# Projections of a hybrid backbone: weight sums on VectorE, the convolution in two buffers loaded a quad ahead, bank copies ahead of its sigmoid

## The chip, the core and the metric

The kernel runs on one core of a Trainium2 chip. The metric is device time in microseconds. The engines are TensorE (PE; its weight loads are PEld), VectorE (DVE), ScalarE (ACT), GpSimd (POOL) and SyncE (SP), which here issues the DMAs of the projections.

## The reference

A two-layer backbone over 256 context and 2048 latent tokens, width 1024, all in float32. In each layer one input projection feeds four head groups, whose outputs are concatenated and projected back. What the change touches is the projection and what is computed beside it:

```
h = rmsnorm(x, norm_g) * (1 + scale) + shift
s = split_cols(h @ w_in)               # 1024 -> all segments, DEPTH = 2 layers
xbc = silu(dwconv_centred(s["ss_xbc"], conv_w, conv_b))    # 3 taps over the tokens, 768 channels
q, k = apply_rope(s["da_q"]), apply_rope(s["da_k"])         # latent tokens
z  = silu(gate segments)
logf, kk = forget gate and key of hg_f, from log_sigmoid
```

## The kernel before

**Products.** `projection(k, l)` runs once a layer. The 18 token tiles are taken in nine pairs, three pairs to a group, and the columns of w_in in five blocks. A *quad* is (group g, block b, member j): one pair of tiles, one block. The order is groups, in them blocks, in them the three members, 45 quads. Each quad is a 2 x 2 block product by seven products instead of eight (Winograd's form): P1 into bank A, P6 into B, P7 into D, P5 into E, then P2 on top of A, P4 on top of D, P3 on top of E. Each product is 4 matmul calls, which the trace shows as 8 instructions. Blocks 0, 1, 2 and 4 have 512 columns (wide quads), block 3 has 268 (narrow quads). In the last layer the context's pair needs plain products of a few columns only; those five quads (0, b, 0) are `simple`.

**Weight sums.** The form needs sums of the four weight quarters: T1 and T2 (`t12`, VectorE, at the end of a block's last quad for the next block), T3 (written over B12; `t3`, GpSimd) and T4 (`t4`, GpSimd). T3 is used by P7, T4 by P4. The sums S1 to S4 of the inputs are GpSimd's (`sums`).

**Bank copies.** ScalarE copies P1 out of bank A (`p1`, L805); only then may TensorE add P2 (its fifth product). When P2 is in, ScalarE copies bank A to the result (L825; L821 in plain quads), and only then may the next quad's P1 start. VectorE adds banks B, D, E and the parts: yy, ff, c22, c21, c12 (L945 to L974). Between them it does, in stages 1 to 4, the elementwise work of the quad before: the forget gate of block 1, the rotation of block 2, the gating.

**Convolution.** The depthwise convolution is cut in 72 jobs over both layers, half of 768 channels by one token tile each. A job is: SP loads three shifted copies of xbc and now and then bias and filter (L497 to L501); GpSimd multiplies and adds in three instructions (L633 to L635); ScalarE makes the sigmoid in three (`conv_gate`: L741, L742, L770); VectorE multiplies into `co` (L967, L978); SP stores (L491). There is one buffer `cx`, and SP loads a job's taps after the product of the job before. `CONV[q]` names the jobs of a quad. They begin in a group's block 1, member 1, and cover all quads to its block 4; some have two.

**Order.** Each engine runs its own instructions in program order and waits on semaphores. In a quad ScalarE does: gates of the quad before, copy L805, `between`, `normalise` where pairs turn, `after`, sigmoid of the quad's first job, copy L825, sigmoid of its second. SP does: the next block's weights (4 MB, first quad of a block, L354), store and taps of the first job, results of the quad before, store and taps of the second.

Of the kernel before, what the change touches and what calls it, by code (L numbers as in the profile page):

```python
# [22 lines left out]
ALU = mybir.AluOpType  # L23
# [3 lines left out]
P = 128  # L27
# [25 lines left out]
XBC = 768  # L53
# [318 lines left out]
def projection(k, l):  # L372
# [30 lines left out]
    CONV_TILES = [range(0, 5), range(5, 11), range(11, NT)]  # L403
    CONV = {q: [] for q in range(N)}
    jobs = []
    for g in range(GROUPS):
        some = [(g, c, t) for c in range(2) for t in CONV_TILES[g]]
        slots = [quad_of[g, b, j] for b in range(1, NB) for j in range(MEMBERS)][1:]
        if g == GROUPS - 1:
            slots = slots[:-1]  # L410
        extra = [quad_of[g, b, j] for b, j in ((3, 0), (3, 1), (3, 2), (4, 0))][:max(0, len(some) - len(slots))]
        for job, q in zip(some, sorted(slots + extra)):
            CONV[q].append(len(jobs))
            jobs.append(job)
# [20 lines left out]
    with ExitStack() as c:  # L435
# [11 lines left out]
        rp = k.sb(c, "rp", [P, NT, 3, 16])  # L447
        cx = k.sb(c, "cx", [P, 4, CWD])
        cw = k.sb(c, "cw", [P, 3, CWD])
        co = k.sb(c, "co", [P, CWD])  # L450
# [6 lines left out]
                      "lf_neg lf_log lf_key kk_ready lf_neg2 lf_log2 lf_done st_u0 st_u1 st_kk taps_in weights_in "  # L457
                      "conv_step conv_sum conv_sig conv_done st_conv act_step dve_step zero_made zero_rows")
# [17 lines left out]
        with nc.Block() as program:  # L476
            @program.sync
            def _(sp):
# [6 lines left out]

                def taps(m):
                    g, c, t = jobs[m]
                    part = slice(c * CWD, c * CWD + CWD)
                    if m:
                        sp.wait_ge(s["conv_done"], m)  # L490
                        sp.dma_start(k.xc[jobs[m - 1][2], :, jobs[m - 1][1] * CWD:(jobs[m - 1][1] + 1) * CWD], co[:]) \  # L491
                            .then_inc(s["st_conv"], 16)
                    q = quad_of[g, 0, 2]
                    sp.wait_ge(s[f"st_u{q % 2}"], stored(q))
                    sp.wait_ge(s[f"st_u{(q - 1) % 2}"], stored(q - 1))
                    for a in range(3):
                        sp.dma_start(cx[:, a], k.xbc[t + 1, a:a + P, part]).then_inc(s["taps_in"], 16)  # L497
                    if m == 0 or jobs[m - 1][1] != c:
# [78 lines left out]
                for q in range(N):  # L577
# [3 lines left out]
                    if CONV[q]:  # L581
                        taps(CONV[q][0])
# [2459 lines left out]
```

## Time and profile before

| | us |
|---|---|
| median of 3 runs | 5803.46 (5801.42 to 5803.72) |
| profiled execution, its own time | 5811.81 |
| its span | 5809.9 |
| PE busy | 5185.6 (89%) |
| DVE busy | 2776.0 (48%) |
| POOL busy | 2750.6 (47%) |
| ACT busy | 1831.9 (32%) |
| mean granted PE clock | 0.935 |
| first to last product, layer 0 | 90.77 to 1191.96 |
| first to last product, layer 1 | 3005.56 to 4123.38 |

The busy share of TensorE is an average over stages. What the projections lose is read from the stretches in which TensorE isn't busy, and from the clock there: 1.00 is 2.4 GHz.

### The profile page before, as it was taken

How to read it: one execution, taken by the hardware profiler on the slowest of the kernel's cores; microseconds unless marked ns; L12 is line 12 of the kernel's file. 1: busy time of each engine (PE TensorE's matmuls, PEld its weight loads, DVE VectorE, ACT ScalarE, POOL GpSimd, SP SyncE). 2: the span in 40 equal slices, each digit the busy share in tenths (PEclk: the TensorE clock that was granted, in tenths of full speed). 3: DMA queues.
4: the chain of work that ended last, by engine and by line, in shares of the span. 5: the costliest groups of instructions: out<-in, count | busy, mean ns of one | idle time of the engine just before them, and what ended most of it. 6: DMA issues, size and time to landing. Idle time of an engine off the chain costs nothing. (4 is left out here: it accounts for less than half of the span.)

```text
span 5809.9 us, 68743 instructions
## 1 busy us (share of the span) xinstructions
PE 5185.6 (89%) x25272; PEld 2736.5 (47%) x25272; DVE 2776.0 (48%) x4578; ACT 1831.9 (32%) x4021; POOL 2750.6 (47%) x1746
## 2 busy tenths in 40 slices
PE   6989899778888899998988898997688879999989
PEld 2454444446777433332434544444467763333334
DVE  2433434335777655551334335353357766555324
ACT  1222222222434244443112222222224432444422
POOL 1333343413344299997113333434134434999941
PEclk8999999877999799998999998998779998999999
DMA  5343433365222100001433333333362211000022
GB/s 185 130 138 131 133 133 130 110 203 176 96 89 75 52 1 8 8 6 71 152 112 121 134 131 127 132 120 110 119 201 83 98 49 46 1 8 8 5 113 104
DMA packets 410015, 559.17 MB, mean 96 GB/s; under 512 B 102840, under 2 KB 281840, under 8 KB 405328
## 3 DMA queue, kind: packets, MB, share of 16 engines
q1 hardware_dynamic: 389954, 514.36, 26.6%
q10 hardware_dynamic: 19728, 40.41, 1.8%
q8 instruction: 203, 3.33, 0.2%
q14 instruction: 130, 1.06, 0.1%
HBM read 400.32 MB, written 154.06 MB: 95 GB/s over the span
## 5 line engine op out<-in xcount | busy, mean ns | idle before, releaser
L2434 POOL TENSOR_TENSOR attention_PS<-attention_PS 128x1024 f32<-128x1024 f32 x548 | 1266.0, 2353 | 80.5 <-ACT attention_PS L2567 73.3
L2480 DVE TENSOR_REDUCE attention_mxp<-psum 128x1 f32<-128x512 f32 (+1 forms) x1016 | 654.7, 686 | 541.9 <-PE psum L2617 541.9
L2567 ACT ACTIVATE attention_PS<-psum 128x512 f32<-128x512 f32 (+1 forms) x1168 | 630.9, 592 | 717.5 <-PE psum L2671 700.3
L2617 PE MATMUL psum<-attention_QK 32*128 32x512 f32 (+1 forms) x2592 | 771.8, 611 | 9.1 <-DVE attention_mxp L2469 6.1
L667 PE MATMUL psum<-group_B,projection_hT 128*128 128x512 f32 (+1 forms) x1360 | 598.6, 587 | 180.9 <-ACT projection_u L825 91.8
L2665 PE MATMUL psum<-attention_QK 32*128 32x512 f32 x2336 | 664.7, 643 | 0.0
L2683 PE MATMUL psum<-attention_PS,attention_va 128*64 128x512 f32 x2336 | 627.7, 616 | 0.0
L667 PE MATMUL psum<-group_B,projection_S 128*128 128x512 f32 (+1 forms) x1360 | 564.2, 558 | 24.6 <-issue 10.4
L667 PE MATMUL psum<-projection_T,projection_S 128*128 128x512 f32 (+1 forms) x1360 | 560.8, 556 | 0.0
L633 POOL TENSOR_TENSOR projection_cx<-projection_cx,projection_cw 128x1152 f32<-128x1152 f32 x72 | 195.6, 2717 | 726.2 <-DMA projection_cx<-xbc 534.1
L667 PEld LDWEIGHTS psum<-group_B,projection_hT 128*128 128x128 f32 x1360 | 276.3, 206 | 464.2 <-issue 393.8
L667 PEld LDWEIGHTS psum<-group_B,projection_S 128*128 128x128 f32 x1360 | 260.9, 192 | 301.2 <-issue 273.9
L667 PEld LDWEIGHTS psum<-projection_T,projection_S 128*128 128x128 f32 x1360 | 262.9, 193 | 273.2 <-issue 260.8
L2665 PEld LDWEIGHTS psum<-attention_QK 32*128 32x128 f32 x2336 | 181.1, 184 | 444.8 <-issue 400.2
L609 POOL TENSOR_TENSOR group_B<-group_B,group_B 128x2048 f32<-128x2048 f32 (+1 forms) x30 | 166.1, 5537 | 407.2 <-DVE projection_T L839 385.9
L1759 POOL TENSOR_TENSOR mixing_Xk<-mixing_E,mixing_hkT 128x256 f32<-128x256 f32 x238 | 191.3, 804 | 314.9 <-ACT mixing_E L1826 307.3
L2617 PEld LDWEIGHTS psum<-attention_QK 32*128 32x128 f32 x2592 | 304.2, 189 | 75.6 <-DVE attention_mxp L2469 42.5
L2683 PEld LDWEIGHTS psum<-attention_PS,attention_va 128*64 128x64 f32 x2336 | 115.9, 135 | 354.3 <-issue 325.1
L667 PE MATMUL psum<-projection_T,projection_hT 128*128 128x512 f32 (+1 forms) x680 | 280.3, 555 | 1.6 <-DVE projection_ff L951 1.6
L2103 PE MATMUL psum<-mixing_mats,mixing_hg 128*128 128x128 f32 x1904 | 280.7, 291 | 0.0
L1826 ACT ACTIVATE mixing_E<-psum 128x512 f32<-128x512 f32 x238 | 141.5, 595 | 414.4 <-PE psum L2103 412.9
L2103 PEld LDWEIGHTS psum<-mixing_mats,mixing_hg 128*128 128x128 f32 x1904 | 235.4, 194 | 29.0 <-issue 0.9
(396 smaller groups left out, 7659.6 us busy)
## 6 DMA issues: line engine op xcount, KB each, us to landing
group_B<-in_w_in SPq DMA_DIRECT2D x120, 512.0 KB, 7.1
group_B<-in_w_in SPq DMA_DIRECT2D x48, 1024.0 KB, 8.9
projection_cx<-xbc SPq DMA_DIRECT2D x216, 192.0 KB, 3.1
u<-projection_u SPq DMA_DIRECT2D x158, 256.0 KB
mixing_hg<-u SPq DMA_DIRECT2D x34, 1024.0 KB, 5.0
u<-projection_u SPq DMA_DIRECT2D x52, 512.0 KB
output_y<-y SPq DMA_DIRECT2D x34, 512.0 KB, 4.1
xc<-projection_co SPq DMA_DIRECT2D x72, 192.0 KB, 2.1
```

Of the source, the lines that this page charges most:

```text
L609: TT(b12[:, :, 0:w], b22[:, :, 0:w], b12[:, :, 0:w], ALU.subtract).then_inc(s["t3_made"], 1)
L633: st.then(TT(cx[:, 0:3], cx[:, 0:3], cw[:], ALU.mult))
L667: ins = nc.tensor.matmul(bank[n][:, 0:w], left[:, q], right[:, q, 0:w], start=(first and q == 0), stop=(q == HK - 1), skip_group_check=True)
L1759: G.tensor_tensor(skew(Xk[v % 2][:], 0, [[w, 2], [2 * w, P // w], [1, w]]), skew(E[v % 2][:], 0, [[256 + w, 2], [2 * w, P // w], [1, w]]), ...
L1826: bk.release(A(out, bk[job][:, 0:w], func), job)
L2103: ins = T(bk[job][:, i * P:(i + 1) * P], hcol(t, "hg_f", i * P, P), m, start=True, stop=True)
L2434: G.tensor_tensor(SA[x % 2][:, rs, 0:w], one[:, rs, 0:w], PT[i % PTB][:, rs, 0:w], ALU.add) \
L2480: bk.release(V.tensor_reduce(mxp[x % 2][:, q:q + nn, 2 * pr + j, a], bk[job, j][:, 0:nn * (hi - lo)].rearrange("p (q n) -> p q n", q=nn), ...
L2567: bk.release(A(PT[i % PTB][:, r, 0:w], bk["st", i, r][:, 0:w], ACT.Exp, scale=scale), ("st", i, r))
L2617: return T(out[:, at:at + hi - lo], QK[rows(r), a0, t * P:(t + 1) * P], QK[rows(r), 2 + a0, lo:hi], start=True, stop=True)
L2665: T(o_, QK[rows(r), 2 + a0, kt * P:(kt + 1) * P], QK[rows(r), a0, t0 * P:(t0 + nq) * P], start=True, stop=False)
L2683: ins = T(k.bank[4 + j][64 * m:64 * m + 64, 0:w], va[:, kts[n], 2 * halves[x][1] + j], PT[i % PTB][:, r, 0:w], start=(n == 0), stop=(n == ...
```

## The change

Three things. T3 and T4 are made by VectorE: T3 of the next block between the bank sums c21 and c12 of a block's last quad, T4 between ff and c22 of a block's first. The convolution gets two buffers and its own table of places, `CONV_SLOTS`; a job's taps are loaded in the quad before it if the job two before is more than a quad back (`ahead`), else in its own quad; VectorE multiplies in place, at the end of the quad; the filter has its own wait. ScalarE copies bank A before all sigmoids of the quad. Beside it the rotation's table is loaded by group, and block 1's stage 2 stands before yy.

```diff
+    CONV_SLOTS.append([(1, 1, 1), (1, 1, 2), (1, 2, 0), (1, 2, 1), (1, 2, 2), (1, 3, 0),
+                       (1, 4, 0), (1, 4, 1), (1, 4, 2), (2, 0, 0), (2, 0, 1), (2, 0, 2)])
+    CONV_SLOTS.append([(2, 1, 1), (2, 1, 2), (2, 2, 0), (2, 2, 1), (2, 2, 2), (2, 2, 2), (2, 3, 0),
+                       (2, 3, 1), (2, 3, 2), (2, 4, 0), (2, 4, 0), (2, 4, 1), (2, 4, 1), (2, 4, 2)])
...
+    new_weights = lambda m: m == 0 or jobs[m][1] != jobs[m - 1][1]
+    new_bias = lambda m: m < 2 or jobs[m][1] != jobs[m - 2][1]
+    ahead = lambda m: m < 2 or at_quad[m - 2] < at_quad[m] - 1
...
-        cx = k.sb(c, "cx", [P, 4, CWD])
+        cx = many("cx", 2, [P, 4, CWD])
...
                 def taps(m):
-                    if m:
-                        sp.wait_ge(s["conv_done"], m)
-                        sp.dma_start(k.xc[...], co[:]).then_inc(s["st_conv"], 16)
...
+                    if m >= 2:
+                        sp.wait_ge(s[f"st_conv{m % 2}"], 16 * (m // 2))
...
+                def weights(m):
+                    at_least(sp, s["conv_sum"], m)
+                    sp.dma_start(cw[:], ...).then_inc(s["weights_in"], 16)
...
-                    if CONV[q]:
-                        taps(CONV[q][0])
+                    for m in CONV[q - 1] if q else ():
+                        conv_store(m)
+                    for m in CONV[q]:
+                        if not ahead(m):
+                            taps(m)
                     if q:
                         store(q - 1)
...
+                    for m in CONV[q + 1] if q + 1 < N else ():
+                        if ahead(m):
+                            taps(m)
+                        if new_weights(m):
+                            weights(m)
...
-                if not last:
-                    t3(0)
                 sums(0)
-                t4(0)
...
-                    for m in CONV[q][:1]:
-                        conv_gate(m)
                     at_least(act, s[f"st_u{q % 2}"], stored(q - 2))
...
                         A(u[q % 2][:, 0, 0:w], bank["A"][:, 0:w], ACT.Copy).then_inc(s["free_A"], 1)
-                    for m in CONV[q][1:]:
+                    for m in CONV[q]:
                         conv_gate(m)
...
+                    if first_of(q) and q:
+                        dve.wait_ge(s["product"], products(q))
+                        t4(i)
...
+                    if last_of(q) and q + 1 < N and not simple(q + 1):
+                        t3(i + 1)
...
+                    for m in CONV[q]:
+                        conv_multiply(m)
```

In the order tables the names are those of the program: p is the copy of P1, e the gates' scratch. ScalarE, layer 0, block 3 of group 1, its first quad and the start of the second; before:

```order
L805 ACTIVATE projection_p<-psum 128x268
L741 ACTIVATE projection_cx<-projection_cx 128x384
L742 ACTIVATE projection_cx<-projection_cx 128x384
L770 ACTIVATE projection_cx<-projection_cx 128x384
L825 ACTIVATE projection_u<-psum 128x268
L741 ACTIVATE projection_cx<-projection_cx 128x384
L742 ACTIVATE projection_cx<-projection_cx 128x384
L770 ACTIVATE projection_cx<-projection_cx 128x384
L741 ACTIVATE projection_e<-projection_u 128x1024
```

The same place now:

```order
L819 ACTIVATE projection_p<-psum 128x268
L837 ACTIVATE projection_u<-psum 128x268
L754 ACTIVATE projection_cx<-projection_cx 128x384
L755 ACTIVATE projection_cx<-projection_cx 128x384
L784 ACTIVATE projection_cx<-projection_cx 128x384
L754 ACTIVATE projection_e<-projection_u 128x1024
```

The copy of bank A (L837) has moved ahead of the sigmoid, and one job instead of two stands in this quad.

SP, layer 0, quad (2,3,0), from the weights of block 4 to the store of the quad before; before:

```order
L354 DMA group_B_3<-in_w_in 128x4x512
L491 DMA xc<-projection_co 128x384
L497 DMA projection_cx<-xbc 128x384 x3
L508 DMA u<-projection_u 128x2x512
L508 DMA u<-projection_u 128x2x256 x2
```

The same place now, on to the filter's load:

```order
L354 DMA group_B_3<-in_w_in 128x4x512
L519 DMA xc<-projection_cx 128x384 x2
L507 DMA projection_cx<-xbc 128x384 x3
L530 DMA u<-projection_u 128x2x512
L530 DMA u<-projection_u 128x2x256 x2
L507 DMA projection_cx<-xbc 128x384 x3
L509 DMA projection_cx<-in_ss_conv_b 128x384
L514 DMA projection_cw<-in_ss_conv_w 128x3x384
```

Two stores stand ahead of the taps of this quad's own job (whose L507 waits for the first of the two to land), and the taps and filter of the next quad's job follow.

VectorE, layer 0, quad (2,3,2), the last narrow quad; now (T3 is written to group_B_1):

```order
L978 TENSOR_TENSOR projection_yy<-psum,projection_p 128x268
L909 TENSOR_TENSOR projection_u<-projection_u,projection_e 128x4x256
L984 TENSOR_TENSOR projection_ff<-psum,projection_yy 128x268
L994 TENSOR_TENSOR projection_u<-psum,projection_ff 128x268
L851 TENSOR_TENSOR projection_T<-group_B_1,group_B_0 128x2048
L854 TENSOR_TENSOR projection_T<-group_B_3,projection_T 128x2048
L1004 TENSOR_TENSOR projection_u<-psum,projection_yy 128x268
L859 TENSOR_TENSOR group_B_1<-group_B_3,group_B_1 128x2048
```

L859 is new on this engine; L851 and L854 (T1, T2) stand where they did.

## Rows read from the trace of the kernel before

**Rows 1.** Line L667: what ended the idle time ahead of it (us, times).

```profile
  ACT projection_u L825: 91.8, 14
...
  ACT projection_p L805: 91.8, 12
```

**Rows 2.** Stretches: length, busy PE, PEld, DVE, ACT, POOL, PEclk, DMA share, GB/s.

```profile
312.31:369.38 57.07, 40.01 (x169) 32.83 (x168) 23.37 (x28) 16.00 (x25) 22.00 (x10) 0.88 0.52 170
664.80:734.01 69.21, 43.45 (x170) 34.63 (x168) 22.32 (x29) 17.45 (x28) 26.52 (x13) 0.83 0.47 152
1027.73:1130.16 102.43, 62.99 (x193) 43.86 (x192) 31.31 (x35) 24.02 (x38) 45.58 (x20) 0.77 0.39 124
3148.49:3180.76 32.27, 13.33 (x42) 8.37 (x41) 20.36 (x16) 9.18 (x13) 13.35 (x5) 0.74 0.51 156
3225.39:3282.78 57.39, 36.87 (x178) 31.59 (x176) 19.14 (x22) 12.66 (x24) 21.45 (x10) 0.76 0.48 158
3584.05:3652.27 68.22, 44.64 (x170) 35.35 (x168) 21.02 (x29) 17.45 (x28) 26.53 (x13) 0.80 0.45 151
3956.97:4061.58 104.61, 63.57 (x193) 43.88 (x192) 30.80 (x35) 24.02 (x38) 45.97 (x21) 0.79 0.38 122
3501.93:3536.00 34.07, 27.05 (x58) 11.26 (x57) 25.78 (x18) 9.60 (x13) 13.94 (x5) 0.90 0.49 149
396.00:664.00 268.00, 268.00 (x662) 121.44 (x661) 103.99 (x122) 67.19 (x120) 89.24 (x38) 1.00 0.35 117
```

**Rows 3.** Timeline of PE, layer 0: start, length, engine, line, operation.

```profile
308.88 3.60 PE L667 MATMUL psum<-group_B,projection_S 128*128 128x512 f32 x8
312.31 1.97 PE L667 MATMUL psum<-group_B,projection_hT 128*128 128x268 f32 x8
314.12 1.97 PE L667 MATMUL psum<-projection_T,projection_S 128*128 128x268 f32 x8
```

**Rows 4.** Timeline of all engines in (2,3,0) and (2,3,1), layer 0.

```profile
1027.92 4.28 SPq L354 DMA_DIRECT2D group_B<-in_w_in  x6
...
1032.25 2.29 SPq L491 DMA_DIRECT2D xc<-projection_co  x1
...
1043.64 2.61 POOL L633 TENSOR_TENSOR projection_cx<-projection_cx,projection_cw 128x1152 f32<-128x1152 f32 x1 [16.64 <-DMA projection_cx<-xbc]
...
1049.23 0.52 ACT L741 ACTIVATE projection_cx<-projection_cx 128x384 f32<-128x384 f32 x1 [16.96 <-POOL projection_cx L635]
...
1051.28 3.91 PE L667 MATMUL psum<-group_B,projection_hT 128*128 128x268 f32 x8 [10.74 <-ACT projection_u L825]
...
1063.47 1.04 ACT L741 ACTIVATE projection_e<-projection_u 128x1024 f32<-128x1024 f32 x1
...
1066.59 0.38 ACT L805 ACTIVATE projection_p<-psum 128x268 f32<-128x268 f32 x1
```

**Rows 5.** DMA from 1027 to 1045 us: total, and issues with KB and us to landing.

```profile
DMA packets 4363, 5.85 MB, mean 325 GB/s; under 512 B 189, under 2 KB 3083, under 8 KB 4363
...
xc<-projection_co SPq DMA_DIRECT2D x1, 192.0 KB, 9.8
```

**Rows 6.** The page's DMA issues, the taps: count, KB, median us to landing.

```profile
projection_cx<-xbc SPq DMA_DIRECT2D x216, 192.0 KB, 3.1
```

**Rows 7.** Line L501, the filter's load.

```profile
DMA to landing us min/median/max: 5.5/6.4/10.6
```

**Rows 8.** Lines L842 (T2), L609 (T3) and L967: count, shortest/median/longest ns.

```profile
L842 DVE TENSOR_TENSOR projection_T<-group_B,projection_T x30: 1274/2292/4594, 74.8 to 4031.4; 128x2048 f32<-128x2048 f32 x24, 128x1072 f32<-128x1072 f32 x6
...
L609 POOL TENSOR_TENSOR group_B<-group_B,group_B x30: 2444/6578/6627, 74.8 to 4051.2; 128x2048 f32<-128x2048 f32 x24, 128x1072 f32<-128x1072 f32 x6
...
L967 DVE TENSOR_TENSOR projection_co<-projection_cx x62: 546/559/4923, 206.7 to 4093.9; 128x384 f32<-128x384 f32 x62
```

**Rows 9.** Timeline, start of layer 0's projection, the first modulation.

```profile
87.00 3.71 DVE L849 TENSOR_SCALAR projection_hT<-psum,projection_G,all_mod 128x256 f32<-128x256 f32 x8 [4.92 <-PE psum L662]
```

**Rows 10.** Timeline, end of the last quad of layer 0, its stores.

```profile
1189.50 4.41 SPq L508 DMA_DIRECT2D u<-projection_u  x3
```

More of the change, by code:

```diff
@@ L493, in taps @@
[L493 to L502 removed]
+                    t = jobs[m][2]
@@ new lines, in taps @@
+                    if m >= 2:
+                        sp.wait_ge(s[f"st_conv{m % 2}"], 16 * (m // 2))
+                    if m == 0 or jobs[m][0] != jobs[m - 1][0]:
+                        q = quad_of[jobs[m][0], 0, 2]
+                        sp.wait_ge(s[f"st_u{q % 2}"], stored(q))
+                        sp.wait_ge(s[f"st_u{(q - 1) % 2}"], stored(q - 1))
+                    for a in range(3):
+                        sp.dma_start(cx[m % 2][:, a], k.xbc[t + 1, a:a + P, part(m)]).then_inc(s[f"taps_in{m % 2}"], 16)
@@ L589, in _ @@
                         load_x(TURN[q] + 1)
-                sp.wait_ge(s["conv_done"], len(jobs))
-                sp.dma_start(k.xc[jobs[-1][2], :, CWD:XBC], co[:]).then_inc(s["st_conv"], 16)
+                for m in CONV[N - 1]:
+                    conv_store(m)
                 store(N - 1)
@@ L594, in _ @@
                     sp.wait_ge(s[f"st_u{q % 2}"], stored(q))
-                sp.wait_ge(s["st_conv"], 16 * len(jobs))
+                for b in range(2):
+                    sp.wait_ge(s[f"st_conv{b}"], 16 * (len(jobs) // 2))
                 sp.wait_ge(s["st_kk"], 16 * of_block(1, N))
@@ L934, in _ @@
                     st.then(V.tensor_tensor(G[:, :, a], G[:, :, a], ng[:], ALU.mult))
+                if not last:
+                    t3(0)
+                t4(0)
                 modulate(0)
                 for q in range(N):
-                    w, v = width(block(q)), u[q % 2]
-                    if q == 1:
-                        dve.wait_ge(s["rope_in"], 16)
+                    w, v, i = width(block(q)), u[q % 2], inst(q)
+                    if q and simple(q - 1):
+                        dve.wait_ge(s["product"], products(q))
+                        t3(i)
                     if q:
                         stage1(q - 1)
+                        if block(q - 1) == 1:
+                            stage2(q - 1)
                     if not simple(q):
@@ L945, in _ @@
                         V.tensor_tensor(yy[:, 0:w], bank["B"][:, 0:w], p1[:, 0:w], ALU.add).then_inc(s["free_B"], 1)
-                    if q:
+                    if q and block(q - 1) != 1:
                         stage2(q - 1)
@@ L951, in _ @@
                         V.tensor_tensor(ff[:, 0:w], bank["D"][:, 0:w], yy[:, 0:w], ALU.add).then_inc(s["ff_made"], 1)
+                    if first_of(q) and q:
+                        dve.wait_ge(s["product"], products(q))
+                        t4(i)
                     if q:
```

120 lines of the change are left out of this document (60 added, 60 removed).

## The prediction, made before the change was run

> **What bounds the kernel now.** I read the totals of the page first. TensorE is busy most of the span, so the question is where it is not. The list of what ended TensorE's idle time in front of the projection's matmuls comes next [rows 1]. The reader is to see that only ScalarE stands there in size: the copy of bank A (L825) and the first copy of it (L805). Then I cut both projections into stretches [rows 2]. From 396 to 664 us TensorE is busy for all 268.00 us at clock 1.00: while products are 512 columns wide, nothing delays it. The time is lost where block 3 comes, with products of 268 columns. From the starts of successive products [rows 3] a wide product takes 312.31 - 308.88 = 3.43 us and a narrow one 314.12 - 312.31 = 1.81 us, so a wide quad of seven costs 24.03 us and a narrow one 12.65 us; three narrow quads cost 37.9 us.
>
> The losses, as stretch minus products [rows 2, 3]:
> - Layer 0, block 3 of group 0: 57.07 - 37.9 = 19.1 us. Group 1: 69.21 - 37.9 = 31.3 us. Group 2, with three wide products behind it that still run late: 102.43 - 37.9 - 10.3 = 54.2 us. Sum 104.6 us.
> - Layer 1, the same places: 57.39 less a plain quad of 8.6 us (64 short matmuls, an estimate from the narrow rate) and two narrow quads of 25.3 us is 23.5 us; 68.22 - 37.9 = 30.3 us; 104.61 - 48.2 = 56.4 us.
> - Layer 1, where the plain quad (0,2,0) hands over: 32.27 us for three products of 3.43 us, loss 22.0 us. Where block 1 hands over to block 2 in groups 1 and 2: 34.07 - 24.03 = 10.0 us, and the second like it, taken as 11 us. Sum for layer 1: 153.2 us.
>
> Together 258 us. This holds idle time and slow clock: the granted clock is 0.74 to 0.90 in these stretches against 1.00 in the clean one, and the narrow product after a gap of 10.74 us takes 3.91 us where its like takes 1.97 us [rows 2 to 4], which is the lower of the two levels (1.2 against 2.4 GHz) and costs 1.9 us a gap.
>
> The mechanism stands in [rows 4], group 2 of layer 0. At 1027.92 SP issues 4 MB of weights, and only then stores the last convolution (1032.25) and loads the taps. They land at 1043.64, when GpSimd starts. Its three steps end at 1049.23, and ScalarE, which had been waiting there, does the sigmoid before the copy of bank A. TensorE needs the bank and starts at 1051.28. A job is a chain of load, three GpSimd steps, three ScalarE steps, VectorE product, store, and one buffer. It takes about 15 us behind weights, longer than a narrow quad.
>
> **The change part by part.**
>
> *Copy before sigmoid.* The bank copy no longer waits for a convolution. The wait isn't gone: it now stands in front of the gates of this quad and the first copy of the next (L805), which TensorE needs at its fifth product. In a narrow quad that is 4 x 1.81 = 7.2 us into the next quad; gates and copy take 1066.59 + 0.38 - 1063.47 = 3.5 us [rows 4], so the sigmoid must end by 3.7 us into the next quad. In a wide quad it is 13.7 us, less some 4 us: by 9 us.
>
> *New places.* Block 3 of group 0 in layer 0 holds no job, that of group 1 one job whose taps are loaded a quad ahead. Both are then free of it: 19.1 + 31.3 + 30.3 us go. In group 0 of layer 1 the jobs are at (0,3,1) and (0,3,2). Taps for the first are issued behind the weights of (0,3,0) and land about 17 us after its start (in group 2 it was 15.7); GpSimd ends at 22.6, the sigmoid at 24, the first copy for (0,3,2) at 27.7, and it is needed at 8.6 + 12.65 + 7.2 = 28.5 us. Just hidden: 23.5 us go. What is late next there is nothing on ScalarE.
>
> *Two buffers, loaded ahead.* A job has its taps ahead only when the job two before is over a quad old. In group 2, (2,2,2) holds two jobs and (2,3,0) the next, so that job is not ahead: SP issues weights, two stores, waits for the first store, and then loads. Start of (2,3,0) is 0. The store is issued at 1032.25 - 1027.73 = 4.5 us and lands 9.8 us later [rows 4, 5]: 14.3 us. Taps need three issues and 3.1 us [rows 6], some 4.4 us: 18.7. GpSimd 5.6 [rows 4]: 24.3. Sigmoid 1.6: 25.9. Gates and first copy 3.5: 29.4. TensorE has got through (2,3,0) and four products, 12.65 + 7.2 = 19.9 us. Gap 9.5 us, and 1.9 us of slow clock: 11.4 us remain, in each layer. The next job's filter is loaded when GpSimd is done with the old one, so its sigmoid ends at 24.3 + 6.4 [rows 7] + 5.6 + 1.6 = 37.9 us, and the first copy of (2,3,2) at 41.4. TensorE, going on at 29.4 with three products of 7.3 us together and then four more of 7.2, wants it at 43.9. Hidden with 2.5 us to spare. So group 2 gives 54.2 - 11.4 and 56.4 - 11.4 = 87.8 us.
>
> The page DMA: Bandwidth & Descriptors of the Trainium skill, section Queues, rings and completion order, says that each DMA engine consumes the descriptors of one issuing queue in ring order. By that, stores issued behind weights wait for them, and the landing of 9.8 us in [rows 5] agrees. Were a short store to pass the weights, the stay would be the short one of the first rival.
>
> *Weight sums to VectorE.* 15 T3 and 15 T4 a projection (T3 of the last layer's plain blocks included), 2.29 us a wide one as T2 takes [rows 8], 1.27 a narrow one. GpSimd took 6.58 at the median. T3 stands in the last quad of a block after c21, and TensorE needs it at the third product of the next quad. In narrow (g,3,2): c22 ends half a microsecond after the fourth product, at about 7.7, T1 and T2 at 12.3, c21 12.7, T3 15.0, needed at 12.65 + 6.9 = 19.5 us. In a wide quad c21 is at 21.3, T3 at 23.6, needed at 30.9. T4 stands after ff in a block's first quad. Wide: ready at 13 us, needed at 17.2. Narrow (g,3,0): rotation and gating end near 8.0 us, T4 at 9.3, and TensorE wants it after five products at 9.03 us: 0.3 us late, up to 2.6 more when a convolution step is in the way. I take 1 us for each of five, 5 us; the ends are 1.5 and 14 us. At the start, T4 and T3 stand ahead of the first modulation: 4.6 us on VectorE against the 4.92 us that it idled there [rows 9], hidden.
>
> *Other side of it.* VectorE is held no more by these long GpSimd steps; an instruction of 0.56 us took up to 4.92 us behind them [rows 8]. At block 1 to 2 in layer 1 that and the earlier second stage make room: c22 comes at about 18.4 us of the 20.6 allowed. I leave 1 us for each of the two: 21.0 - 2 = 19 us. At (0,2,0) the chain stays: copy, a negation, two ScalarE steps, three VectorE steps, T4 of 2.29, two more, two ScalarE steps, copy, with some 1.2 us for each VectorE step (half the length of T2) and 1.1 for each of ScalarE's (as 1063.47 in [rows 4]) about 15.8 us against 7.2 us of products. 8.6 + 2.6 us of slow clock remain of 22.0: 10.8 us go.
>
> *Tail.* The last job moves into the last quad. Its store, and the three of the last quad behind it on SP, are issued after the last VectorE product; before, two of the three went while products ran, from 1189.50 [rows 10]. About 2 us later in each layer: +4 us, between 1 and 6.
>
> Sum: 19.1 + 31.3 + 30.3 + 23.5 + 87.8 + 19 + 10.8 - 5 - 4 = 212.8 us. On the profiled execution's own 5811.8 us that is 5599 us. The median of the runs is 8.35 us below that execution, so 5590.6; I say 5591 us.
>
> **The rivals.**
>
> *Nothing remains in group 2.* The stores land in 2 to 3 us, the taps by 12 us, the sigmoid by 19: no gap. The DMA queue is against it, moving 5.85 MB at 325 GB/s from 1027 to 1045 [rows 5]. 22.8 us better, and 5 for T4: 5563 us.
>
> *The late load spreads.* One filter load of 6.4 us had 10.6 at worst [rows 7]. Then the sigmoid in (2,3,1) ends at 42 and a second gap of 2 us and slow clock follow; block 3 of group 0 in layer 1, which had 0.8 us to spare, opens a gap of 5 too. With as much again in the third quad, some 30 us worse: 5621 us.
>
> *The shared port.* GpSimd now works through its jobs whenever taps are there, and 60 more VectorE steps read two SBUF operands. If each of them, and the rotation beside it, waits out one 2.6 us step where TensorE waits too, half of them cost 30 x 2.6 = 78 us: 5669 us. For it: VectorE's product took up to 4.92 for 0.56, T2 4.59 for 2.29 [rows 8]. Against it: T3 and T4 in wide quads have 4 to 7 us of slack. The page SBUF — State Buffer of the Trainium skill, section Who interferes with whom, says that a VectorE instruction with two SBUF inputs and a GpSimd one that reads SBUF exclude each other for a whole instruction, and that the one issued first wins; the trace agrees with that.
>
> *Slower.* One mechanism: the first copy (L805) now stands behind the previous quad's sigmoid. If jobs came so late that it missed TensorE at all of them, the gain of 258 us would have to be eaten by 72 jobs, 3.6 us each; that needs GpSimd's sums later than about 7.4 us into the quad after their own, for all jobs in wide quads too. They come some 10 to 22 us into their own quad. Priced at 4 us each: 5833 us.
>
> *The change does not do what it says* would be the taps not ahead; in six of 14 jobs of group 2 they aren't, which is in the sum.
>
> **How the numbers follow.** Forecast 0.55, nothing remains 0.12, late load spreads 0.17, port 0.11, slower 0.03; 0.02 for a mix in which all cancels. What a measurement of this kernel can tell from no change is about 0.2%, 12 us. Range: from just under the first rival to just over the third, 5552 to 5680; beyond it lie the slower case and some of the port's. Faster 0.95, same 0.02, slower 0.03.
>
> **What would show it.** In the new profile: stretches of block 3 in groups 0 and 1 at 38 to 40 us and clock near 1.00; L825's new line gone from what TensorE waited for; one gap of 8 to 11 us in (2,3,1) in front of the fifth product, released by the first copy, in each layer; a gap of 8 to 9 us after (0,2,0) in layer 1; VectorE's share up by some 120 us, GpSimd's down by about 300. Wrong would be gaps in wide quads, or TensorE waiting for T3, T4 or VectorE's bank sums by more than some 10 us in all.

## The result, and the profile after

The changed kernel takes 5593.38 us (median of 4 runs, 5589.37 to 5595.73) against 5803.59 us before on the same chip (4 runs, 5801.42 to 5805.06). The ratio is 0.9637, with a 95% interval of 0.9621 to 0.9654. Its profiled execution took 5593.15 us, with a span of 5591.3 and a mean granted clock of 0.947 (before 0.935). The prediction was 5591 us.

The page's totals of the changed kernel, busy time by engine:

```profile
PE 5134.1 (92%) x25238; PEld 2711.6 (48%) x25272; DVE 2815.2 (50%) x4638; ACT 1830.4 (33%) x4021; POOL 2478.7 (44%) x1686
```

The next rows list, for one group of matmuls in each kernel, busy time, mean length, and the idle time of TensorE ahead of them with what ended it. First before, then after (L667 has become L680, L825 is L837, L805 is L819, L821 is L833):

```profile
L667 PE MATMUL psum<-group_B,projection_hT 128*128 128x512 f32 (+1 forms) x1360 | 598.6, 587 | 180.9 <-ACT projection_u L825 91.8 <-ACT projection_p L805 44.6 <-ACT projection_u L821 36.7
```

```profile
L680 PE MATMUL psum<-group_B,projection_hT 128*128 128x512 f32 (+1 forms) x1360 | 567.0, 561 | 36.1 <-ACT projection_p L819 20.0 <-ACT projection_u L833 8.6 <-DVE projection_hT L875 7.6
L680 PE MATMUL psum<-group_B,projection_S 128*128 128x512 f32 (+1 forms) x1360 | 556.3, 552 | 2.3 <-DVE projection_u L994 2.3
```

The bank A copy has gone from the list, and 180.9 us of idle time have become 36.1. The mean matmul is shorter too, 561 ns for 587, since fewer come at the low clock behind a gap. These rows count matmuls alone. The view of [rows 1] counts the weight loads of the line too, so its 91.8 us for L805 are 44.6 us of TensorE's idle time in six gaps, each counted a second time for the weight load beside it; no term of the sum used that number.

The stretches of the changed kernel that answer to [rows 2] (length, busy PE, PEld, DVE, ACT, POOL, granted clock, DMA share, GB/s): block 3 of groups 0 and 1 in layer 0, the clean stretch, and of group 2 the quad (2,3,0) with six of the seven products of (2,3,1).

```profile
312.00:350.20 38.20, 38.20 (x170) 31.84 (x169) 19.05 (x28) 11.63 (x16) 0.00 (x0) 1.00 0.61 199
643.85:682.00 38.15, 38.15 (x169) 31.83 (x168) 19.48 (x29) 13.08 (x19) 0.00 (x0) 1.00 0.60 199
396.00:664.00 268.00, 268.00 (x691) 128.17 (x690) 118.13 (x138) 71.08 (x122) 69.56 (x38) 1.00 0.42 142
975.69:1012.00 36.31, 25.27 (x100) 20.31 (x99) 13.11 (x21) 9.24 (x14) 11.30 (x6) 0.81 0.69 231
```

57.07 and 69.21 us have become 38.20 and 38.15 us at clock 1.00; three narrow quads without any wait were put at 37.9. Only group 2 still waits there. In TensorE's timeline these are the gaps inside the two projections that cost most (start, length, operation, then the idle time before and its releaser):

```profile
1007.02 3.94 PE L680 MATMUL psum<-group_B,projection_hT 128*128 128x268 f32 x8 [11.04 <-ACT projection_p L819]
...
3073.11 5.73 PE L680 MATMUL psum<-group_B,projection_hT 128*128 128x512 f32 x8 [8.57 <-ACT projection_u L833]
...
3814.95 3.54 PE L680 MATMUL psum<-group_B,projection_hT 128*128 128x268 f32 x8 [8.91 <-ACT projection_p L819]
```

The others of over 1 us are two of 1.16 and 1.15 us for c22 (L994) where block 1 hands over to block 2 in layer 1, and one of 3.80 us for the modulation (L875) at the start of layer 1, which stands in the kernel before too. The first of the three rows above, with what leads to it, in the timeline of all engines; (2,3,0) starts at 975.69:

```profile
975.88 4.82 SPq L354 DMA_DIRECT2D group_B<-in_w_in  x6
...
980.75 2.37 SPq L519 DMA_DIRECT2D xc<-projection_cx  x2
...
991.91 1.27 SPq L507 DMA_DIRECT2D projection_cx<-xbc  x3
...
996.34 2.61 POOL L657 TENSOR_TENSOR projection_cx<-projection_cx,projection_cw 128x1152 f32<-128x1152 f32 x1 [31.48 <-DMA projection_cx<-xbc]
...
1001.93 0.52 ACT L754 ACTIVATE projection_cx<-projection_cx 128x384 f32<-128x384 f32 x1 [16.56 <-POOL projection_cx L659]
...
1003.47 1.04 ACT L754 ACTIVATE projection_e<-projection_u 128x1024 f32<-128x1024 f32 x1
...
1005.94 2.62 POOL L657 TENSOR_TENSOR projection_cx<-projection_cx,projection_cw 128x1152 f32<-128x1152 f32 x1 [4.04 <-DMA projection_cw<-in_ss_conv_w]
...
1006.59 0.38 ACT L819 ACTIVATE projection_p<-psum 128x268 f32<-128x268 f32 x1
```

It reads as in [rows 4], with another engine at the end: SP issues weights, then two stores; its queue waits 8.8 us for the first store to land; then come the taps, GpSimd, the sigmoid, the gates of the quad, and the copy that TensorE's fifth product needs.

From the first to the last product, layer 0's projection took 1101.4 us before and 1009.6 us after, layer 1's 1118.0 and 991.8: 91.8 + 126.2 = 218.0 us, less what came later behind them (below). (Here the end is that of the last matmul; the table of the kernel before counts 0.2 us less in each layer.) The stages that the change doesn't touch differ by some 4 us between the two executions.

### The profile page after: what moved, and what is told of

It reads as the page before. It is cut to its first block and busy times, and to the rows that moved or that the text cites. A ratio compares the mean times of both kernels' runs of the same rounds, so it can differ in the third digit from the quotient of the medians.

```text
span 5591.3 us, 68589 instructions
## 1 busy us (share of the span) xinstructions
PE 5134.1 (92%) x25238; PEld 2711.6 (48%) x25272; DVE 2815.2 (50%) x4638; ACT 1830.4 (33%) x4021; POOL 2478.7 (44%) x1686
## 5 line engine op out<-in xcount | busy, mean ns | idle before, releaser
L680 PE MATMUL psum<-group_B,projection_hT 128*128 128x512 f32 (+1 forms) x1360 | 567.0, 561 | 36.1 <-ACT projection_p L819 20.0
L680 PE MATMUL psum<-group_B,projection_S 128*128 128x512 f32 (+1 forms) x1360 | 556.3, 552 | 2.3 <-DVE projection_u L994 2.3
L680 PE MATMUL psum<-projection_T,projection_S 128*128 128x512 f32 (+1 forms) x1360 | 556.1, 551 | 0.0
L680 PEld LDWEIGHTS psum<-group_B,projection_hT 128*128 128x128 f32 x1360 | 261.9, 194 | 303.1 <-issue 263.1
L680 PEld LDWEIGHTS psum<-group_B,projection_S 128*128 128x128 f32 x1360 | 258.2, 190 | 273.0 <-issue 259.3
L680 PEld LDWEIGHTS psum<-projection_T,projection_S 128*128 128x128 f32 x1360 | 258.4, 190 | 270.0 <-issue 260.2
L837 ACT ACTIVATE projection_u<-psum 128x512 f32<-128x512 f32 (+1 forms) x85 | 47.2, 555 | 754.7 <-PE psum L680 754.7
L680 PE MATMUL psum<-projection_T,projection_hT 128*128 128x512 f32 (+1 forms) x680 | 279.5, 554 | 1.2 <-DVE projection_ff L984 0.9
```

What stands on the lines that cost most here:

```text
L680: ins = nc.tensor.matmul(bank[n][:, 0:w], left[:, q], right[:, q, 0:w], start=(first and q == 0), stop=(q == HK - 1), skip_group_check=True)
```

## Experiments

Twelve kernels ran, each beside the kernel before on its own chip (medians of before 5804 to 5810 us). "Of before" and "of changed" say from which kernel the edit starts; interval always means 95%. The next table collects them; sum means the time of both projections, first to last product, in the profiled execution; "by the traces" below means by this column. The medians of before differ by up to 6 us between the groups of runs, and a difference of two medians carries that. The intervals of a3, a4, c1 and b3 overlap the changed kernel's; there the traces have to decide.

| run | edit | us | ratio to before (interval) | sum |
|---|---|---|---|---|
| before | | 5803.6 | 1 | 2219.4 |
| changed | | 5593.4 | 0.9637 (0.9621 to 0.9654) | 2001.4 |
| s2 | of before: new places | 5680.6 | 0.9788 (0.9773 to 0.9802) | 2094.7 |
| s1 | of changed: old places | 5652.0 | 0.9739 (0.9725 to 0.9754) | 2064.3 |
| a1 | of before: copies first | 5785.7 | 0.9969 (0.9957 to 0.9982) | 2200.8 |
| a2 | of before: T3, T4 on VectorE | 5781.4 | 0.9968 (0.9955 to 0.9981) | 2191.4 |
| c2 | of before: copies first, product last | 5780.3 | 0.9948 (0.9936 to 0.9960) | 2188.1 |
| a3 | of changed: T3, T4 on GpSimd | 5609.6 | 0.9658 (0.9645 to 0.9672) | 2014.4 |
| a4 | of changed: sigmoid before copy | 5603.9 | 0.9650 (0.9637 to 0.9663) | 2013.8 |
| c1 | of changed: product early | 5601.9 | 0.9643 (0.9631 to 0.9656) | 2010.4 |
| b2 | of changed: never ahead | 5616.3 | 0.9671 (0.9658 to 0.9684) | 2023.8 |
| b1 | of changed: one job moved | 5576.7 | 0.9600 (0.9587 to 0.9614) | 1984.2 |
| b3 | of changed: plain copies early | 5589.4 | 0.9623 (0.9610 to 0.9636) | 1995.9 |
| b4 | b1 and b3 | 5577.8 | 0.9599 (0.9586 to 0.9613) | 1981.5 |

**The places, alone and undone.** s2 gives the kernel before the new table; s1 gives the changed kernel the old rule.

```diff
-        for job, q in zip(some, sorted(slots + extra)):
-            CONV[q].append(len(jobs))
+        for slot, (c, t) in zip(CONV_SLOTS[g], itertools.product(range(2), CONV_TILES[g])):
+            CONV[quad_of[slot]].append(len(jobs))
```

> The kernel before with the new places of the convolution's jobs and nothing else: one buffer, sigmoid ahead of the bank copy, T3 and T4 on GpSimd. My theory, that the loss was jobs standing in narrow quads behind the weights' load: block 3 of group 0 (layer 0) free, of group 1 one gap instead of three, of group 2 about half, the plain quads of layer 1 free of jobs: 135 us of the 210 us gained, 5669 us (5640 to 5700). Rival, that two buffers loaded ahead and the copy's order carry it: under 50 us gained, above 5750 us.

> The changed kernel with the old places, all else as changed. My theory: layer 0's group 0 stays free (all jobs ahead), group 1 has one gap of some 10 us at its doubled narrow quad, group 2 with two jobs in each narrow quad stays at some 36 us of loss instead of 13; the same in layer 1: 78 us slower than changed, 5671 us (5640 to 5700). Rival, that the buffers and the order make the places indifferent: below 5610 us.

s2 measured 123 us below before, 12 us less than its forecast. s1 came to 58.6 us above the changed kernel, where 78 was forecast. The miss of s1 lies in group 2: block 3 and the first quad behind it lose 26.9 us in layer 0 and 28.5 in layer 1 (stretch less undisturbed products), where 36 was forecast. In s2 block 3 of groups 0 and 1 and that of group 2 with the quad behind it lose 0, 12.4 and 23.1 us in layer 0, where the kernel before loses 19.1, 31.3 and 54.2; the hand-overs from block 1 to 2 in layer 1 stay at 10.0 and 11.0 us. The places are the largest part, but what they are worth depends on the rest: 123 us in the kernel before, 59 in the changed one. With the old places, gaps come back in block 3, as this one of s1 in group 1, layer 0, in TensorE's timeline:

```profile
675.74 3.94 PE L677 MATMUL psum<-group_B,projection_hT 128*128 128x268 f32 x8 [11.94 <-ACT projection_p L816]
```

**The order of ScalarE alone.** a1 is the kernel before with this:

```diff
-                    for m in CONV[q][:1]:
-                        conv_gate(m)
                     at_least(act, s[f"st_u{q % 2}"], stored(q - 2))
...
-                    for m in CONV[q][1:]:
+                    for m in CONV[q]:
                         conv_gate(m)
```

> The kernel before, only the bank copies ahead of all sigmoids of the quad. My theory: the wait moves to the first copy of the next quad (L805), so where jobs come behind the weights the gap of some 10 us stays and only changes its releaser; won are about 6 us in group 0, 11 us and 8 us at the plain quads of layer 1: 27 us, 5776 us (5755 to 5790). Rival, that the copy's order was the stall as the list of releasers suggests (92 us by the bank copies): 90 us or more gained, below 5715 us.

It gained 18 us, not 27. The releasers of a1, in the same groups as above:

```profile
L667 PE MATMUL psum<-group_B,projection_S 128*128 128x512 f32 (+1 forms) x1360 | 582.9, 574 | 106.5 <-DVE projection_u L970 56.8 <-issue 39.7 <-DVE projection_u L956 10.0
L667 PE MATMUL psum<-group_B,projection_hT 128*128 128x512 f32 (+1 forms) x1360 | 575.6, 568 | 77.8 <-ACT projection_p L805 61.1 <-ACT projection_u L819 9.0 <-DVE projection_hT L847 7.7
```

The bank A copy has gone, as wanted, and 56.8 us of c21 (L970 here) have come. VectorE's product of the convolution stood ahead of c21, and waits for the same sigmoid. The change had moved it behind c12; that is in its text, but no term of the prediction priced it.

A third queue shows itself in the same rows: 39.7 us of "issue", where the kernel before had 10.4. All of it stands at third products, which need T3. T3 is GpSimd's here, and ahead of the three largest of these gaps (14.02, 12.76 and 9.87 us) it stands behind the steps of a late job. The largest, in the timeline of all engines:

```profile
1111.28 0.99 POOL L635 TENSOR_TENSOR projection_cx<-projection_cx 128x384 f32<-128x384 f32 x1
1112.23 4.51 POOL L609 TENSOR_TENSOR group_B<-group_B,group_B 128x2048 f32<-128x2048 f32 x1
...
1116.85 6.48 PE L667 MATMUL psum<-group_B,projection_S 128*128 128x512 f32 x8 [14.02 <-issue]
```

T3 (L609) ends at 1116.74, and TensorE starts 0.11 us later. After the other gaps of this kind (12.76, 9.87, 2.12 and 0.96 us in layer 1) TensorE starts as close behind a T3.

Two more runs price the product's place. c1 puts the product back in the changed kernel, c2 adds its move to a1. c1's edit:

```diff
                         modulate(TURN[q])
+                    for m in CONV[q][:1]:
+                        conv_multiply(m)
                     if q:
                         stage4(q - 1)
...
-                    for m in CONV[q]:
+                    for m in CONV[q][1:]:
                         conv_multiply(m)
```

> The changed kernel with one thing put back: VectorE's product of a quad's first convolution stands ahead of the bank sums c21 and c12 again, not behind them. Theory (the place of this product is a part of the change of its own, which the prediction did not price): in (2,3,0) the sigmoid ends at 1003.56; behind it come the product (0.56), a gating step and c21, so bank D is free at about 1004.8, and TensorE wants it at the third product of (2,3,1), 12.65 + 3.6 us after 975.69, that is 991.9. The gap moves from the fifth product to the third, and the fifth starts at about 1010 and not at 1007.0: 3 us in each layer, and 1 to 2 us at (0,3,1) of layer 1: 5593 + 8 = 5601 us (5597 to 5607), with 12 to 13 us of idle ahead of the third product of (2,3,1), released by VectorE's c21 (L994 or the like). Rival, the product's place is indifferent, since the first copy of the next quad ends last anyway: 5593 us (5589 to 5596), and the gap stays at the fifth product.

> The kernel before with two edits of order: ScalarE's bank copies ahead of all sigmoids, and VectorE's product of a quad's first convolution behind the bank sums c21 and c12. The first edit alone gave 5785.7 us and left 120.6 us of TensorE's idle time to c21 and 124.7 us to the first copy. Theory: the two belong together; without the wait of VectorE the third product starts in time and only the fifth waits, for the first copy, which comes 3 to 4 us before the time at which the fifth starts now, at five places in each layer, and the smaller gaps of c21 go: 20 to 35 us, so 5760 us (5748 to 5772), c21 under 30 us in the list and the first copy above 124.7. Rival, the sigmoid's lateness passes on in full to the first copy (ScalarE is the real end of the chain): 5786 us (5780 to 5790).

c1 measured 5601.9 us. Its projections take 9.0 us longer than the changed kernel's, and its gap stands where the theory put it, at the third product and released by c21, in the timeline of TensorE (the second row is the fifth product, which had started at 1007.02):

```profile
1004.25 3.94 PE L680 MATMUL psum<-group_B,projection_S 128*128 128x268 f32 x8 [11.32 <-DVE projection_u L1006]
...
1010.29 1.97 PE L680 MATMUL psum<-group_B,projection_hT 128*128 128x268 f32 x8
```

The loss isn't where the theory put it, though: not 3 us in each layer, but 0.3 us in layer 0 and 8.7 in layer 1. In layer 0 TensorE restarts earlier in c1, with two products more to do: the seventh product of (2,3,1) starts within 0.2 us of the changed kernel's, both counted from the first product. In layer 1 c1 loses 2.4 us up to (0,3,2), 2.0 at group 2's hand-over from block 1 to 2, and 3.3 from (2,3,1) on. So the price of the product's place is paid in layer 1.

c2 missed: 5780.3 us where 5760 was expected and 5786 by the rival. Its releasers:

```profile
L667 PE MATMUL psum<-group_B,projection_hT 128*128 128x512 f32 (+1 forms) x1360 | 580.7, 572 | 147.2 <-ACT projection_p L805 127.6 <-ACT projection_u L819 11.9 <-DVE projection_hT L847 7.7
L667 PE MATMUL psum<-group_B,projection_S 128*128 128x512 f32 (+1 forms) x1360 | 563.2, 557 | 45.1 <-issue 43.0 <-DVE projection_u L956 2.2
```

c21 is out, and its 56.8 us stand almost whole in the first copy, 61.1 become 127.6. Freed of one wait, TensorE only runs up to the next that hangs on the same late job, and T3 on GpSimd is one of them: of the 43.0 us of "issue", 38.9 are three gaps right behind a T3. So the order of ScalarE and VectorE is worth little while jobs are late: 18 us, then 5 more by the medians, 12 by the ratios and 13 by the traces (the intervals of a1 and c2 just overlap). Both orders together with the sums on VectorE, at the old places, were not run. In the changed kernel, where few jobs are late, the order is worth 10.5 us for ScalarE (a4; 12.4 by the traces) and 8.5 us for VectorE (c1; 9.0 by the traces).

**The sums alone and undone.** a2 gives the kernel before T3 and T4 on VectorE, a3 gives the changed kernel's back to GpSimd. The core of a2:

```diff
-                    if last_of(q) and q + 1 < N:
-                        if not simple(q + 1):
-                            t3(inst(q + 1))
-                        produced(gp, q, "P4")
-                        t4(inst(q + 1))
...
+                    if first_of(q) and q:
+                        dve.wait_ge(s["product"], products(q))
+                        t4(i)
...
+                    if last_of(q) and q + 1 < N and not simple(q + 1):
+                        t3(i + 1)
```

> The kernel before, only T3 and T4 on VectorE. My theory: it takes away what GpSimd's long steps did to VectorE at block 1 to 2 in layer 1 (15 of 21 us) and the late T3 of group 2's block 4 (some 7 us in each layer), and leaves the narrow quads: 30 us, 5773 us (5760 to 5790). Rival, shared port and a fuller VectorE: no gain or slower, 5800 us or more.

> The changed kernel with T3 and T4 back on GpSimd. My theory: block 1 to 2 in layer 1 loses some 12 us again, T3 of block 4 in group 2 a few us: 20 us slower, 5613 us (5600 to 5625). Rival, that VectorE's share is what now costs at the start of narrow blocks: within 5 us of changed.

Minus 22 us alone (30 were expected), and plus 16 undone (20 were expected; 13 by the traces). In a3 the gap behind the plain quad (0,2,0) is 12.75 us where the changed kernel has 8.57, and gaps of 1.09 to 1.57 us come where block 1 hands over to block 2; narrow blocks lose at most 1 us. In the changed kernel the sums are worth moving for layer 1 alone: a3's layer 0 is no longer than the changed kernel's. In the kernel before they are worth 8.9 us in layer 0 too, 5 of them at the T3 of group 2's block 4.

The two runs also show that the hand-overs from block 1 to 2 in layer 1, which lost 21.0 us before and 3.5 after, owe the smaller part to the weight sums: a2 still loses 5.0 and 9.2 us there, a3 only 4.0 and 3.9. The rest must come from other parts of the change. The prediction named the second stage of block 1, now ahead of yy; no run has that alone, so it is not shown.

**The first sigmoid ahead of the copy again.** a4, of the changed kernel:

```diff
+                    for m in CONV[q][:1]:
+                        conv_gate(m)
                     at_least(act, s[f"st_u{q % 2}"], stored(q - 2))
```

> The changed kernel with the first job's sigmoid ahead of the bank copy again. My theory: only where the job is late, at (2,3,0) in each layer (TensorE stops before the first product of (2,3,1) instead of the fifth, some 4 us more) and at (0,3,1) of layer 1 (some 4 us): 12 us slower, 5605 us (5600 to 5615). Rival, that the order carries the change: 50 us slower or more.

Plus 10.5 us, nearly all of it in layer 1 (0.9 us in layer 0, 11.4 in layer 1). TensorE now waits for the bank A copy at three places: 13.28 us at the start of (2,3,1) in layer 0 (at 1001.62) and 13.44 in layer 1, and 3.79 us at (0,3,2) of layer 1 (at 3152.44), behind the job that the prediction called just hidden there.

**Taps never a quad ahead, and one job moved.** b2 and b1, of the changed kernel:

```diff
-    ahead = lambda m: m < 2 or at_quad[m - 2] < at_quad[m] - 1
+    ahead = lambda m: False
```

```diff
-    CONV_SLOTS.append([(2, 1, 1), (2, 1, 2), (2, 2, 0), (2, 2, 1), (2, 2, 2), (2, 2, 2), (2, 3, 0),
+    CONV_SLOTS.append([(2, 1, 1), (2, 1, 2), (2, 2, 0), (2, 2, 1), (2, 2, 1), (2, 2, 2), (2, 3, 0),
```

> The changed kernel with two buffers, but every job's taps loaded in its own quad. My theory: only jobs of narrow quads notice, (1,3,0) opens a gap of some 7 us and 2 us of slow clock in each layer, and a few us come in (2,3,1), (2,3,2) and at (0,3,1) of layer 1: 27 us slower than changed, 5620 us (5605 to 5635). Rival, that the loads ahead carry the gain in wide quads too: 80 us slower or more.

> The changed kernel with one number changed: in group 2 the quad with two jobs is (2,2,1) instead of (2,2,2), so that the job of (2,3,0) has its taps ahead. My theory of the rest that the changed kernel loses (11.04 and 8.91 us of gap in (2,3,1), and slow clock behind them, because taps wait for a store that waits for the weights): both gaps go, 24 us, 5569 us (5563 to 5577). Rival, that the filter's load or ScalarE's work makes the gap: it stays at (2,3,1) or moves one quad, less than 8 us gained.

b2 loses 23 us, near its forecast: gaps of 6.14 and 6.45 us come in block 3 of group 1, which holds one job, and the gaps for c22 at the two hand-overs in layer 1 grow from 1.2 to 2.99 and 3.34 us. b1 gains 17 us of the 24 expected (its interval lies wholly below the changed kernel's). With the pair of jobs one quad earlier, (2,3,0)'s job gets its taps ahead, and the gaps of 11.04 and 8.91 us are gone. What is left comes a quad later, released by the same copy behind the next job:

```profile
1010.81 2.07 PE L680 MATMUL psum<-group_B,projection_hT 128*128 128x268 f32 x8 [1.78 <-ACT projection_p L819]
...
3807.68 3.65 PE L680 MATMUL psum<-group_B,projection_hT 128*128 128x268 f32 x8 [2.40 <-ACT projection_p L819]
```

**The plain quad's copies ahead of the steps of the quad before.** b3, of the changed kernel, and b4 with b1's edit added:

```diff
+                    early = simple(q) and q not in TURN
+                    if early:
+                        plain_copies(q)
                     if q:
                         between(q - 1)
```

> The changed kernel, in which ScalarE copies the plain products of a plain quad (unless pairs turn in it) before the key's exponential and the second log, which wait for VectorE's stages of block 1. My theory of the gap of 8.57 us before (0,2,1) in layer 1: it is this chain and nothing in TensorE's way needs it, so the gap goes but for 1 us: 10 us, 5583 us (5579 to 5588). Rival, that the banks are free late for another reason (VectorE's): under 3 us gained.

> The changed kernel with the double job at (2,2,1) and the early plain copies. If both gaps are independent they add up: 5593 - 24 - 10 = 5559 us (5553 to 5566). If one hides the other, more than 5569 us.

b3 should have given 10 us and gave about 4 by the medians, 8 by the ratios and 5.5 by the traces. The gap of 8.57 us is gone and another stands two products on. VectorE and TensorE in b3's timeline:

```profile
3057.87 2.28 DVE L872 TENSOR_TENSOR projection_T<-group_B,projection_T 128x2048 f32<-128x2048 f32 x1
...
3065.91 2.28 DVE L867 TENSOR_TENSOR group_B<-group_B,group_B 128x2048 f32<-128x2048 f32 x1
...
3068.29 6.07 PE L680 MATMUL psum<-group_B,projection_S 128*128 128x512 f32 x8 [4.75 <-issue]
```

The third product needs T3 (L867), which stands on VectorE behind block 1's stages: it ends at 3068.19, and TensorE starts at 3068.29. "Issue" as releaser hides this: the cause is read from what ended 0.1 us before. b4 missed its 5559 us and can't be told from b1; with the 17 us that b1 gave and the 4 of b3, 5572 was to be expected, and its four executions lie between 5569 and 5584. Whether T3 ahead of the stages would give the rest was not tried.

## Why the prediction was right

**Groups 0 and 1, block 3 (104.2 us).** Right in place and size: both stretches of layer 0 are at 38.2 us and clock 1.00, and no gap of over 1 us stands in block 3 of groups 0 and 1. The job in (0,3,1) of layer 1 was near its limit, as said: TensorE waited 0.90 us for ff in (0,3,2), at 3156.50.

**Group 2 (87.8 us).** The mechanism is the predicted one. Block 3 with what follows it still loses 14.1 us in layer 0 and 10.9 in layer 1, where 11.4 each were forecast. Steps from the start of (2,3,0), predicted and measured: store landed 14.3 and 16.2; taps 18.7 and 20.7; sigmoid starts 24.3 and 26.2; it ends 25.9 and 27.8; first copy done 29.4 and 31.3. The store is the mis-sized one, by 1.9 us, the rest follows it (the taps took 0.1 us more than forecast). The changed kernel's DMA issues in this stretch (count, KB, median us to landing), and what SP's queue waited for there (us, times, longest):

```profile
xc<-projection_cx SPq DMA_DIRECT2D x2, 192.0 KB, 10.4
```

```profile
SPq L507 <- DMA xc<-projection_cx: 8.8, 1, 8.8
```

As in [rows 5], stores issued behind the weights stay long, 10.4 us here for 1.9 at the page's median. So the gap was 11.04 us in layer 0 where 9.5 was forecast, and 8.91 in layer 1. The slow clock cost 3.94 + 2.69 - 2 x 1.97 = 2.7 us in layer 0 and 3.54 - 1.97 = 1.6 in layer 1, where 1.9 each was forecast. Together 24.2 us stayed where the sum had 22.8. GpSimd waited 4.0 us for the next job's filter where 6.4 was forecast, so the slack of (2,3,2) was not used, and the rival of the late load that spreads had no ground.

**VectorE's sums.** T4 in narrow first quads came almost in time, as in (0,3,0) of layer 0, in the timeline of the changed kernel:

```profile
319.23 1.97 PE L680 MATMUL psum<-group_B,projection_hT 128*128 128x268 f32 x8
...
319.87 1.26 DVE L864 TENSOR_TENSOR projection_T<-group_B,projection_T 128x1072 f32<-128x1072 f32 x1
...
321.19 2.07 PE L680 MATMUL psum<-projection_T,projection_hT 128*128 128x268 f32 x8
```

The fifth and sixth products stand 1.96 us apart instead of 1.81, and T4 ends at 321.13. That is 0.15 us late at each of the five places, under 1 us in all where I took 5. Busy time rose by 2815.2 - 2776.0 = 39 us, not by 120. The rows that show why, VectorE in the kernel before and in the changed one (count, busy, mean ns):

```profile
L967 DVE TENSOR_TENSOR projection_co<-projection_cx 128x384 f32<-128x384 f32 x62 | 89.0, 1436 | 224.7 <-ACT projection_cx L770 224.7
...
L882 DVE TENSOR_TENSOR projection_u<-projection_u,projection_e 128x512 f32<-128x512 f32 (+1 forms) x68 | 80.7, 1186 | 5.6 <-ACT projection_e L765 5.3
L842 DVE TENSOR_TENSOR projection_T<-group_B,projection_T 128x2048 f32<-128x2048 f32 (+1 forms) x30 | 69.2, 2305 | 1.0
```

```profile
L859 DVE TENSOR_TENSOR group_B<-group_B,group_B 128x2048 f32<-128x2048 f32 (+1 forms) x30 | 69.6, 2320 | 27.9 <-PE psum L699 27.8
...
L854 DVE TENSOR_TENSOR projection_T<-group_B,projection_T 128x2048 f32<-128x2048 f32 (+1 forms) x30 | 63.3, 2111 | 1.0
...
L864 DVE TENSOR_TENSOR projection_T<-group_B,projection_T 128x2048 f32<-128x2048 f32 (+1 forms) x30 | 62.3, 2078 | 0.0
L909 DVE TENSOR_TENSOR projection_u<-projection_u,projection_e 128x512 f32<-128x512 f32 (+1 forms) x68 | 61.8, 909 | 5.1 <-ACT projection_e L778 4.8
L868 DVE TENSOR_TENSOR projection_cx<-projection_cx 128x384 f32<-128x384 f32 x72 | 54.6, 765 | 29.4 <-ACT projection_cx L784 29.4
```

The new steps cost 69.6 + 62.3 = 131.9 us, and others got shorter by 93: the convolution's product (from 1436 to 765 ns on average; the first row has 62 of the 72), the gating (from 1186 to 909), T2 (from 2305 to 2111). a3 tells how much of this the sums did: with them back on GpSimd VectorE is busy for 2755.7 us, 72 more than the changed kernel without its new steps (2815.2 - 131.9 = 2683.3), and the product takes 1299 ns on average. The gating (950) and T2 (2111) stay short in a3, so another part of the change shortened them; which one was not tried. GpSimd went from 2750.6 to 2478.7 us, 272 less for 300. The prediction named this relief beside the sum and then forgot it in its count of busy time. The port rival (5669 us) erred the other way: with 293 us of long GpSimd steps gone, VectorE is blocked less, not more. The rule of the Trainium skill that it rested on (SBUF — State Buffer, Who interferes with whom) says that the one that issues first holds the shared pair for its whole instruction. By that rule, taking GpSimd's long steps away shortens VectorE's stalls, and the 72 us of a3 agree. The rival priced the steps that came to VectorE and left out those that went from GpSimd.

**Layer 1's hand-overs (29.8 us).** Forecast 8.6 us of gap and 2.6 of slow clock behind (0,2,0); measured 8.57 and 5.73 - 3.60 = 2.13. Block 1 to 2: forecast 1 us each, measured 1.16 + 0.33 and 1.15 of gaps, and 2.0 and 1.5 us as stretch less undisturbed products. The total was right. The prediction did not say how it divides between shorter waits behind GpSimd and the earlier second stage; by a2 and a3 the sums are the smaller part.

**The tail.** From the last product to the next stage's first work on TensorE: 10.91 us before, 12.84 after in layer 0, 10.95 and 13.15 in layer 1; 4.1 us, forecast 4.

**The start.** Hidden, as forecast: the first product of layer 0 starts at 90.40 us, before at 90.77.

**What is luck in the number.** The forecast of 5591 us stands 2.4 us from the median. The sum gave 212.8 us, and the projections with their tails gave 218.0 - 4.1 = 213.9. Of the terms, T4's was 4 us too high; what was to remain in group 2 was 2.2 us too low, and at the hand-overs from block 1 to 2 1.5 us. The stages outside the projections took some 4 us less, for which there was no term. The median was put 8.35 us below the profiled execution, as before; the changed kernel's lies 0.2 us above it. These two errors cancel in part, and by luck: on the profiled execution's own time the forecast was 5599, and it took 5593.15.

**What was not in the steps.** The place of VectorE's product is worth 8.5 us (c1) and had no term. The sum took the stretches' losses as gone where no job was late, and so held it unseen: without that move it would have been 8.5 us too good. Likewise the parts don't add up: places, order of ScalarE and sums alone give 123 + 18 + 22 = 163 us of 210. The other 47 come from parts together, or from parts that were not tried alone: the two buffers, the filter's own wait, the rotation's table, the second stage of block 1. One way in which parts help each other is shown: the order of the copies alone lets 29.3 us more of waits for T3 appear (39.7 for 10.4), and the changed kernel, with few late jobs and T3 on VectorE, has none. How the rest divides stays open.

The version to keep is b1, 5576.7 us: it beats both kernels, the changed one by 17 us (0.9600 against 0.9637, the intervals apart).

## What to carry to other kernels

A job that hangs on a late load holds every engine whose queue it stands in, and taking it out of one queue passes the wait on to the next: a1 and c2 moved some 60 us from ScalarE's copy to VectorE's sum and back to ScalarE, and some 30 us to GpSimd's T3, and gained 18 us and 5 to 13. First make the job early (its place, its buffer, its load), then order the engines. And price a loss by stretch length less the undisturbed spacing, step by step through one instance of the wait; then look at each instruction that the diff moves in each queue, also where the reason for the move isn't told. A releaser "issue" is not an answer: look for what ended 0.1 us before.

## What was not expected of the hardware

- Taking 60 GpSimd steps of up to 6.6 us away and adding 60 on VectorE of up to 2.3 us raised VectorE's busy time by 39 us only; its other steps got 93 us shorter, and 72 of these came back in a3, with the sums on GpSimd again (2755.7 us).
- Two stores of 192 KB behind 4 MB of weights took 10.4 us to land at the median, against 1.9 for all 72. The filter load (L514), 5.9 us at the median of its 12, held GpSimd for 4.04 us one quad later.
- After a gap of 11.04 us TensorE ran one narrow product in 3.94 us and the next in 2.69 before it was back at 1.97; after the one of 8.91 us it ran one in 3.54 and was back. After the 8.57 us gap a wide product took 5.73 for 3.60, and the next was back at 3.60. After gaps of 0.3 to 1.2 us wide products took 3.70.
